# Softmax inside a projection GEMM: who divides the probabilities by their sums, and where the reciprocal stands

## The reference, cut to what matters

```python
def one_block(q_blk):
    s = jnp.einsum('bqhgd,bkhd->bhgqk', q_blk, k).astype(jnp.float32) * scale
    p = jax.nn.softmax(s, axis=-1).astype(v.dtype)
    return jnp.einsum('bhgqk,bkhd->bqhgd', p, v)
...
h = modulate(rmsnorm(x, norm1_g[l]), sh1, sc1)
p = h @ w_in_l
...
o = block_attention(q, k_all, v_all)
y = merge_branches(o, p[..., V_END:F_END], p[..., F_END:], w_attn_o[l], w_fourier[l], w_out[l])
...
x = x + g1 * y
h2 = modulate(rmsnorm(x, norm2_g[l]), sh2, sc2)
x = x + g2 * sq_relu_mlp(h2, w1[l], w2[l])
```

## Time and profile before

| | us |
|---|---|
| median of 3 runs | 1509.71 (1509.41 to 1510.2) |
| the profiled execution | 1509.67 |
| its span, first to last instruction | 1507.8 |
| PE busy / VectorE busy / ScalarE busy | 1476.0 / 990.0 / 665.7 |
| the attention units stand at | about 294 to 553 |

### The profile page before, as it was taken

The page is one execution under the profiler, slowest core; times in us unless marked ns, Lnnn a source line. Parts: engine busy times, 40 slices in busy tenths (PEclk is TensorE's granted clock), DMA queues, the critical chain, the costliest instruction groups (busy, mean ns, idle before and its releaser), DMA issues.

```text
span 1507.8 us, 19480 instructions
## 1 busy us (share of the span) xinstructions
PE 1476.0 (98%) x7361; PEld 1217.8 (81%) x7361; DVE 990.0 (66%) x1151; ACT 665.7 (44%) x904; POOL 49.6 (3%) x33
## 2 busy tenths in 40 slices
PE   5999999999999999999999999999999999999997
PEld 2567888888888888888888888888888888888886
DVE  2455865867667678997777568778756455555456
ACT  3322543555545453344454444444434444444443
POOL 0000100101000000010100000000200000000000
PEclk9999999999999999999999999999999999999999
DMA  9997775664667679879665577788555656555552
GB/s 368 358 357 261 279 242 192 214 217 155 224 208 239 206 240 335 314 282 371 232 224 153 164 267 270 266 303 279 195 183 200 194 192 194 195 194 192 190 192 95
DMA packets 123180, 355.73 MB, mean 236 GB/s; under 512 B 11106, under 2 KB 12130, under 8 KB 122466
## 3 DMA queue, kind: packets, MB, share of 16 engines
q1 hardware_dynamic: 121492, 353.43, 68.8%
q10 hardware_dynamic: 1616, 1.31, 0.3%
HBM read 352.60 MB, written 2.10 MB: 235 GB/s over the span
## 4 chain that ended last, share of the span: by engine, by line
PE 89%; DVE 5%; issue 2%; ACT 2%; DMA 1%; ACTq 0%; POOL 0%; POOLq 0%; DVEq 0%; SPq 0%
PE bank L1542 21%; PE bank L1544 20%; PE bank L1543 20%; PE bank L1817 14%; PE bank L1820 7%; PE bank L1702 2%; PE bank L1674 1%; DVE wl L1111 1%; ACT wh L691 1%; PE bank L1574 1%; DVE acc L1142 1%; PE bank L1664 1%; DMA ident<-in_identity 1%; PE bank L1627 0%; DVE mx L1235 0%
## 5 line engine op out<-in xcount | busy, mean ns | idle before, releaser
L1111 DVE TENSOR_TENSOR wl<-raw,wh 128x1024 fp32r<-128x1024 f32 x452 | 560.0, 1250 | 371.0 <-ACT wh L691 369.9
L691 ACT ACTIVATE wh<-raw 128x1024 fp32r<-128x1024 f32 x452 | 473.8, 1059 | 474.4 <-PE bank L1544 286.2
L1817 PE MATMUL bank<-h2S,wh 128*128 128x512 f32 x896 | 245.0, 395 | 0.1
L1542 PE MATMUL bank<-wh,hT 128*128 128x512 f32 x512 | 207.7, 406 | 3.3 <-DVE wl L1111 1.3
L1544 PE MATMUL bank<-wh,hT 128*128 128x512 f32 x512 | 200.4, 391 | 0.0
L1543 PE MATMUL bank<-wl,hT 128*128 128x512 f32 x512 | 200.0, 391 | 0.0
L1544 PE MATMUL bank<-wh,hidS 128*128 128x512 f32 x496 | 193.2, 389 | 0.0
L1542 PE MATMUL bank<-wh,hidS 128*128 128x512 f32 x496 | 193.2, 389 | 0.0
L1543 PE MATMUL bank<-wl,hidS 128*128 128x512 f32 x496 | 193.2, 389 | 0.0
L1817 PEld LDWEIGHTS bank<-h2S,wh 128*128 128x128 f32 x896 | 153.3, 189 | 20.7 <-DVE hs L1391 0.5
L1142 DVE SCALAR_TENSOR_TENSOR acc<-raw,cc,acc 128x1024 f32<-128x1024 f32 x120 | 153.5, 1279 | 0.0
(11 more groups left out here) (221 smaller groups left out, 1597.8 us busy)
## 6 DMA issues: line engine op xcount, KB each, us to landing
raw<-in_w SPq DMA_DIRECT2D x256, 512.0 KB, 3.8
raw<-in_w_ada SPq DMA_DIRECT2D x192, 512.0 KB, 5.6
raw<-in_w_in SPq DMA_DIRECT2D x128, 512.0 KB, 4.5
raw<-in_w_attn_o SPq DMA_DIRECT2D x32, 512.0 KB, 5.9
raw<-in_w_out SPq DMA_DIRECT2D x32, 512.0 KB, 5.9
raw<-in_w_fourier SPq DMA_DIRECT2D x16, 512.0 KB, 6.3
xt<-in_x SPq DMA_DIRECT2D x2, 1024.0 KB, 6.1
ct<-in_ctx SPq DMA_DIRECT2D x2, 1024.0 KB, 10.7
```

The costliest lines, as they stand in the source:

```text
L691: nc.scalar.activation(slot, raw[:, s % RAW, :], ACT.Copy).then_inc(wh_done, 1)
L1111: nc.vector.tensor_tensor(lo, raw[:, s % RAW, :], hi.bitcast(F32), ALU.subtract)\
L1542: nc.tensor.matmul(bank[b][:], a_hi, w_hi, start=first, stop=False)
L1817: nc.tensor.matmul(out[:].rearrange("p (v t) -> p v t", v=2), wh[:, slot, cols_f[f]], h2S[:, :, block, :], start=(block == 0), stop=False)
```

## The change

The reciprocal of unit u-1 moves on VectorE from behind the maximum of unit u to ahead of it, and loses its `then`. The multiplication by it leaves VectorE; ScalarE does it as a Copy with the reciprocal as its scale, in the slot of unit u, ahead of that unit's exponentials. ScalarE waits for a new semaphore, `rinv_ready`. All other work keeps its place.

```diff
@@ scalar, post(m)
                 if m in SLOTS:
                     u = SLOTS[m]
+                    if 1 <= u < UNITS + 1:
+
+                        w = u - 1
+                        act.wait_ge(rinv_ready, w + 1)
+                        nc.scalar.activation(probs[:, w % 2, :], probs[:, w % 2, :], ACT.Copy, scale=rinv[:, w:w + 1])\
+                            .then_inc(pn_ready, 1)
                     if u < UNITS:
@@ vector, post(m)
                     u = SLOTS[m]
+                    if 1 <= u < UNITS + 1:
+                        w = u - 1
+                        dve.wait_ge(exp_done, w + 1)
+                        nc.vector.reciprocal(rinv[:, w:w + 1], rsum[:, w:w + 1]).then_inc(rinv_ready, 1)
                     if u < UNITS:
...
                         nc.vector.tensor_tensor(nb[:, u:u + 1], mx[:, u:u + 1], nqs[:, h // 8, col:col + 1], ALU.mult)\
                             .then_inc(nb_ready, 1)
-                    if 1 <= u < UNITS + 1:
-                        w = u - 1
-                        dve.wait_ge(exp_done, w + 1)
-                        then(nc.vector.reciprocal(rinv[:, w:w + 1], rsum[:, w:w + 1]))
-                        nc.vector.tensor_scalar(probs[:, w % 2, :], probs[:, w % 2, :], rinv[:, w:w + 1], None, ALU.mult)\
-                            .then_inc(pn_ready, 1)
```

More of the change, by code:

```diff
@@ L457, in block_program @@
         hi_done = sem("hi_done")
+        rinv_ready = sem("rinv_ready")
         k_hi = sem("k_hi")
```

## The result

| | before | changed |
|---|---|---|
| median of 20 runs each, us | 1509.63 | 1511.55 |
| span of the profiled execution, us | 1507.8 | 1509.9 |
| VectorE busy / ScalarE busy, us | 990.0 / 665.7 | 973.4 / 688.2 |

The ratio of the times is 1.0013, with a 95% interval of 1.0007 to 1.0019: 1.9 us more, against a forecast of 1511.6. The change is smaller than the 3.0 us that the prediction took as the least that a measurement can tell, but with 20 runs of each kernel the interval lies wholly above no change. Of the ten executions of one kernel further down (the Copy behind the gate banks) one took 3840.8 us; nothing recorded says why, and it has no part in the ratio given there.

The account below looks back on a forecast made before the run. The prediction took the PE to bound the kernel, with a VectorE-ScalarE loop delaying it in two stretches of the stage. 1509.67 + 0.7 (reciprocals) + 1.2 (Copy at gate ends) = 1511.6 us, range 1509.0 to 1514.9.

Parts of the forecast that it names:

- What bounds: Whole span: PE busy 98%; in the stage between 294 and 553 us only stretches where PE waits for side engines count.
- the loop: VectorE and ScalarE in the stage: maximum, exponentials, rounding, split, next maximum; the chain runs through it 301.73-318.08 and 329.90-383.24.
- 318.71 and 383.24: Times in us at which the loop gives the PE its start, each by way of a bank that ScalarE empties.
- The removal: VectorE's multiplication, 16.2 us in all, lies wholly in a hole before a split that waits for ScalarE; worth nothing.
- Nine reciprocals: Reciprocals ahead of maxima on the chain through the loop, 0.075 us each: 0.7 us, bounds 0 and 1.7.
- my row with a split behind a small operation: Trace row behind the reciprocal's price: a 0.16 us instruction pushes the next start by 0.07 to 0.08, 407.13 to 407.20.
- The price of 0.156 each: Alternative for the nine reciprocals, next operation starting only when the pipe is empty: 1.4 us, sum 0.7 higher; not adopted.
- The Copy under the maximum: ScalarE's Copy in ordinary slots, costing its engine 0.62 us, fits beneath VectorE's maximum with 0.18 us left; costs nothing.
- Two gate ends: Units 19 and 27, where exponentials don't wait for VectorE: Copy delays gate bank release, 2 x 0.62 = 1.2 us, bounds 0.8-1.9.
- What would show it: Signs: VectorE busy down about 16 us, ScalarE up about 23, gate weight loads waiting 0.9 instead of 0.27 us.
- The sum of 1.9: Whole kernel: 0.7 us for reciprocals plus 1.2 for the Copy at gate ends, 1.9 over the profiled execution and median.

Follow-up runs that it names:

- the Copy behind the gate banks: Changed kernel with the Copy of units 10, 18 and 26 behind the last two gate banks; 1509.96 us against 1509.4 before, ratio 0.9993 to 1.0013.
- without any division: Kernel before with the multiplication left out, probabilities not divided by their sums; 1510.01 us against 1509.72 before, ratio 0.9994 to 1.0012.
- alone: Kernel before with only the reciprocal moved ahead of the maximum, VectorE still multiplying; 1509.66 us against 1509.4 before, ratio 0.9992 to 1.0011.
- the kernel with five: Changed kernel with four more reciprocals between the first one and the maximum; 1513.23 us against 1509.4 before, ratio 1.0016 to 1.0039.
- Two Copies: Changed kernel with a second Copy in place behind the first, for which it waits; 1518.88 us against 1509.4 before, ratio 1.004 to 1.0074.
- the two profiled executions of one kernel: Kernel before with ScalarE's two copies of a unit, transposed probabilities and output, one tile later; 1506.67 us against 1509.72 before, second run 1507.45 against 1509.86.

## Why the prediction was right

- **What bounds.** Right: the chain through the loop up to the first gate group and through gate banks behind it is what moved, and nothing behind the stage did. The prediction named two places where the loop gives the PE its start, 318.71 and 383.24, and missed a third: the weight load that waits for a split at 365.42, 0.51 us before and 0.74 (at 365.86) in the changed kernel. Its delay comes from reciprocals that are among the nine, so the sum did not suffer.
- **The removal, costed at nothing.** Right, and shown: without any division the stage is as long.
- **Nine reciprocals, 0.7 us.** The count is right, the price 0.06 instead of 0.075: 0.52 us in the changed kernel, 0.56 alone, 0.060 each in the kernel with five. The maximum itself got 0.01 us shorter behind a reciprocal (0.67 for 0.68), which my row with a split behind a small operation could not show. The price of 0.156 each, weighed there by a rule of the Trainium skill (VectorE: DVE Perf Modes, section The DRAIN you can't avoid), did not come, and I had read only half of that rule: the section adds that a next operation that is not held starts earlier. The trace agrees with that half, 0.06 to 0.08 us from start to start.
- **The Copy under the maximum, costed at nothing.** Right, with the size of its cover. From the Copy's start to that of the exponentials it is 0.79 us; ScalarE would have been free after 0.62, so 0.17 are left (forecast 0.18). Two Copies used it up.
- **Two gate ends, 1.2 us.** Right: 0.62 and 0.65 by the scores, 0.61 each by the waits of the weight loads, and given back when the Copy stood behind the banks.
- **What would show it.** One sign was worded wrongly. I had said that the exponentials still wait for VectorE at 29 or 30 units; the rows show 7 such waits, and 29 at the Copy ahead of them. They start just when the scaled maximum lets them; the list of waits puts idle time down to the first instruction behind it. The distance between maxima in the loop grew by 0.05 to 0.06, a little less than the 0.07 to 0.08 named.
- **Chance in it.** The sum of 1.9 was 0.1 too high for the stage (1.8), and the medians differ by 1.9 with an interval of 1.1 to 2.9. That 1511.6 met 1511.55 so closely is luck in the last tenths.

## What to carry to other kernels

Between two engines that hand work back and forth, busy time said nothing here; draw the loop, and put each instruction either in it or in a hole. The multiplication in its hole was free on VectorE. On ScalarE it was free beneath the maximum, and at the gate ends behind the last two banks. It cost something at the other places that were tried: behind the exponentials in the loop, ahead of a bank that the PE waits for, and so late that the PE waited for it. When a loop of this kind binds, look for work in it that nobody in the loop needs: here it was two copies that belonged behind the next rounding, worth 2.3 us where the division's move cost 1.8.

## What the runs showed of the hardware

- A VectorE instruction on 128x1 is 0.15 to 0.16 us long in the trace and pushes the next one back by 0.06 to 0.08, also five in a row.
- A 128x512 float32 Copy with a scale from SBUF is 0.72 us long on ScalarE and costs it 0.62. The multiplication was 0.51 on VectorE in the mean, 0.49 in the median. Both lengths are above my estimates by the Trainium skill (VectorE: DVE Perf Modes, section The TRN2 errata), 0.61 and 0.33. The 0.61 fits the Copy without a scale, 0.614 long in the earlier trace rows; of its figures for VectorE the same section says that they come out too low.
- In the two profiled executions of one kernel the last scores stand within 0.1 us of each other, counted from the first (234.33 and 234.29), while the stage as a whole starts 1.2 us apart.
